# Expert weights in a ring of sixteen 1 MB slots, expert loops unrolled by four, and the slot pick moved behind the transposes of the hidden layer

## The reference

```
gt  = min(x @ w_gate[e] + b_gate[e], 7)
up  = clip(x @ w_up[e] + b_up[e], -7, 7)
out = ((up + 1) * gt * sigmoid(1.702 * gt)) @ w_down[e] + b_down[e]
```

## Time and profile before

| | |
|---|---|
| runs | 1501.61, 1501.67, 1499.98 us; median 1501.61 |
| the profiled execution | 1499.89 us, of which the span is 1498.0 us |
| PE busy | 1383.3 us (92%), 6703 instructions |
| DVE, ACT busy | 584.5 us (39%), 287.7 us (19%) |
| mean granted TensorE clock | 0.948 of 2.4 GHz |
| DMA | 445.40 MB, mean 297 GB/s; expert weights 192 DMAs of 2048 KB |

### The profile page before, as it was taken

One profiled execution on the slowest core, in us unless ns is written; L12 is line 12 of the kernel. 1 busy time (PEld: TensorE's weight loads), 2 busy tenths in 40 slices (PEclk: granted clock), 3 DMA queues, 4 the chain that ended last, 5 costly groups with the idle time before them and its releaser, 6 DMA issues.

```text
span 1498.0 us, 18536 instructions
## 1 busy us (share of the span) xinstructions
PE 1383.3 (92%) x6703; PEld 598.1 (40%) x6704; DVE 584.5 (39%) x1195; ACT 287.7 (19%) x484; POOL 4.0 (0%) x24
## 2 busy tenths in 40 slices
PE   7997778997699999999999999999999999999993
PEld 5886565686233333333333333333333333333331
DVE  2998687311433233433334233412333332222231
ACT  2132222012112212212112212111112211121111
POOL 0000000000000000000000000000000000000000
PEclk9999787598799999999999999999999999999996
DMA  9343112233099999999999999976899998777550
GB/s 395 145 183 120 56 44 109 102 154 137 10 412 417 414 399 400 416 415 416 405 392 416 417 415 401 416 300 262 351 414 417 415 415 339 280 313 301 217 233 30
DMA packets 35404, 445.40 MB, mean 297 GB/s; under 512 B 4904, under 2 KB 5288, under 8 KB 8624
## 3 DMA queue, kind: packets, MB, share of 16 engines
q1 hardware_dynamic: 33760, 443.20, 72.1%
q10 hardware_dynamic: 1616, 1.82, 0.3%
HBM read 437.80 MB, written 7.20 MB: 297 GB/s over the span
## 4 chain that ended last, share of the span: by engine, by line
PE 81%; DVE 10%; DVEq 3%; issue 3%; ACT 2%; DMA 0%; ACTq 0%
PE ps L1203 51%; PE ps L1180 6%; PE ps L1213 6%; DVE acts L586 5%; PE ps L986 3%; PE ps L1193 2%; DVEq L587 2%; PE ps L1102 2%; PE ps L1146 2%; PE ps L1086 2%; PE ps L1093 1%; PE ps L1010 1%; PE ps L1220 1%; ACT extra L513 1%; PE ps L1064 1%
## 5 line engine op out<-in xcount | busy, mean ns | idle before, releaser
L1203 PE MATMUL ps<-ring,extra 128*64 128x512 f32 x3360 | 778.7, 604 | 0.0
L1203 PEld LDWEIGHTS ps<-ring,extra 128*64 128x64 f32 x3360 | 223.0, 137 | 447.5 <-issue 447.5
L901 DVE TENSOR_TENSOR acts<-ps,acts 128x528 f32<-128x528 f32 x132 | 93.4, 708 | 511.9 <-PE ps L1213 511.9
L1180 PE MATMUL ps<-acts 128*64 128x512 f32 (+1 forms) x432 | 105.4, 607 | 2.9 <-issue 2.9
L518 ACT ACTIVATE extra<-extra 128x512 f32<-128x512 f32 x64 | 39.4, 630 | 352.7 <-DVE extra L906 352.7
L1213 PE MATMUL ps<-acts,extra 64*128 64x264 f32 x576 | 100.7, 433 | 4.5 <-DVE acts L901 2.4
L586 DVE SCALAR_TENSOR_TENSOR acts<-acts,small 128x256 f32<-128x256 f32 x240 | 102.7, 479 | 5.1 <-ACT acts L401 0.7
L1213 PEld LDWEIGHTS ps<-acts,extra 64*128 64x128 f32 x576 | 44.6, 186 | 112.0 <-issue 107.4
L529 ACT ACTIVATE extra<-ps 128x512 f32<-128x512 f32 x64 | 34.7, 594 | 249.4 <-PE ps L1203 249.4
L513 ACT ACTIVATE extra<-ps 128x512 f32<-128x512 f32 x66 | 36.2, 595 | 221.6 <-PE ps L1180 221.6
L1010 PE MATMUL ps<-acts,ring 128*128 128x280 f32 (+1 forms) x320 | 77.2, 401 | 0.3 <-DVE acts L661 0.3
(11 more groups left out here) (243 smaller groups left out, 823.3 us busy)
## 6 DMA issues: line engine op xcount, KB each, us to landing
ring<-in_w_experts SPq DMA_DIRECT2D x192, 2048.0 KB, 12.2
ring<-in_w_in_t SPq DMA_DIRECT2D x5, 2048.0 KB, 21.0
extra<-in_w_in_t SPq DMA_DIRECT2D x4, 2048.0 KB, 11.1
ring<-in_state_t SPq DMA_DIRECT2D x8, 512.0 KB, 17.4
extra<-in_w_out_t SPq DMA_DIRECT2D x4, 1024.0 KB, 5.9
ring<-in_w_out_t SPq DMA_DIRECT2D x4, 1024.0 KB, 5.8
out_ssm_s_t<-ring SPq DMA_DIRECT2D x8, 512.0 KB, 2.6
acts<-in_x_cm SPq DMA_DIRECT2D x2, 560.0 KB, 5.8
```

The costliest lines, as they stand in the source:

```text
L901: TT(both, ps[:, 6:8, 0:TN], both, ALU.add).then_inc(ev["acc_done"], 1)
L1180: h = MM(dst, S[0:r, j, HALF * b:HALF * (b + 1)], xn[0:r, j, 512 * h_:512 * (h_ + 1)], start=(j == 0), stop=(j == 2))
L1203: hs.append(MM(dst, src[:, o:o + HALF], piece(p)[:, k, 512 * h_:512 * (h_ + 1)], start=(fresh and kk == 0), stop=(kk == KT - 1), skip_grou ...
```

## The change

- SBUF is laid out anew: `ring` and `acts` become one tensor `main`; the router's tables, `gfin` and the like move from `acts` to `small`, so that the first 32 KB of `acts` are free for four more slots once the mixer is over. The twelve pieces of an expert now go round sixteen slots: piece p of an expert with i mod 4 = s lies in slot (12 s + p) mod 16. Loads keep their trigger events, but go four pieces further ahead; the first two pairs of expert 1 are loaded with expert 0's last ones.
- As slots depend on i mod 4, the expert loops of TensorE and SP have four experts in their body (8 passes on TensorE; SP: 7 passes and 3 experts written out).
- TensorE: `pick_slots` goes from between up pieces 5 and 6 to between `turn_hidden` and `turn_following`. The wait for `xg_out` is by block, and `down_of` waits for it too.
- ScalarE: the order is `inputs_out` b, `hidden_out` b for b = 0, 1, then `gates_out`. VectorE: `hidden` comes before `Pm`.
- POOL's iota waits for `wo_used` instead of two earlier events.

```diff
-        NP = 12
-        ring = sb("ring", NP * PIECE)
+        NP, SLOTS = 12, 16
+        main = sb("main", NP * PIECE + 16400)
+        ring, acts = main, main[:, NP * PIECE:NP * PIECE + 16400]
         extra = sb("extra", 4 * PIECE)
-        acts = sb("acts", 16400)
-        small = sb("small", 4000)
+        small = sb("small", 4040)
...
+        def slot_of(s, p):
+
+            return (NP * s + p) % SLOTS
...
+            sp.wait_ge(ev["yvar_mm"], 1)
+            for q in range(2):
+                sp.dma_start(pair_row(6 + q), expert_pair(1, q)).then_inc(landed[6 + q], 16)
...
-            with sp.Fori(0, NE - 1) as i:
-                sp.wait_ge(ev["gate_used"], i + 1)
-                for q in range(2):
-                    sp.dma_start(pair_row(q), expert_pair(i + 1, q)).then_inc(landed[q], 16)
-                for q in range(2, NP // 2):
-                    sp.wait_ge(ev["piece_used"], i * 8 + 2 * q - 2)
-                    sp.dma_start(pair_row(q), expert_pair(i + 1, q)).then_inc(landed[q], 16)
+            def load_next(e, s, last=False):
+
+                for q in range(2, 6):
+                    if q < 4:
+                        sp.wait_ge(ev["gate_used"], e)
+                    else:
+                        sp.wait_ge(ev["piece_used"], e * 8 + (2 * q - 14))
+                    pair = slot_of(s, 2 * q) // 2
+                    sp.dma_start(pair_row(pair), expert_pair(e, q)).then_inc(landed[pair], 16)
+                if not last:
+                    for q in range(2):
+                        sp.wait_ge(ev["piece_used"], e * 8 + (2 * q - 2))
+                        pair = slot_of(s + 1, 2 * q) // 2
+                        sp.dma_start(pair_row(pair), expert_pair(e + 1, q)).then_inc(landed[pair], 16)
+
+            with sp.Fori(0, NE // 4 - 1) as ii:
+                for s in range(1, 5):
+                    load_next(ii * 4 + s, s)
+            for e in range(NE - 3, NE):
+                load_next(e, e % 4, e == NE - 1)
...
             with a.Fori(0, NE) as i:
                 sigmoid(i * 2)
+                for b in range(2):
+                    inputs_out(i * 2 + 2, b)
+                    hidden_out(i * 2, b)
                 gates_out(i)
-                inputs_out(i * 2 + 2)
-                hidden_out(i * 2)
                 output_out(i)
...
                 choose_slots(i + 2).then_inc(ev["s_ready"], 1)
+                hidden(i, i * 2)
                 v.wait_ge(ev["gp_ready"], i + 1)
                 for b in range(2):
                     h = STT(Pm[:, b, :], ps[:, 6, 0:TN], slot_id[:, b:b + 1], gp, ALU.is_equal, ALU.mult)
                 h.then_inc(ev["p_ready"], 1)
                 choose_bias(i + 2).then_inc(ev["oh_ready"], 1)
-                hidden(i, i * 2)
...
-                    if p == 5:
-                        pe.wait_ge(ev["acc_done"], n4 + 4)
-                        pick_slots()
...
                         if p == 8:
                             pe.wait_ge(ev["ht_ready"], i2 + 1 + b)
+                            pe.wait_ge(ev["xg_out"], i2 + 3 + b)
...
-                by_width(count, lambda n: up_of(n, i * 16 + 16, i * 4))
+                def turn_following(n):
+                    for b in range(n):
+                        pe.wait_ge(ev["xg_out"], i * 2 + 3 + b)
+                        if b:
+                            pe.wait_ge(ev["hdn_ready"], i * 2 + 2)
+                    turn(n, xg, 2, ev["xt_done"])
+
+                by_width(former, lambda n: gate_of(n, s, i48, former_rows))
+                by_width(count, lambda n: up_of(n, s, i48))
                 pe.wait_ge(ev["s_ready"], i + 2)
-                by_width(following, lambda n: gather(n))
+                by_width(following, gather)
                 by_width(count, lambda n: turn_hidden(n, i * 2))
-                pe.wait_ge(ev["xg_out"], i * 2 + 4)
+                pe.wait_ge(ev["acc_done"], i * 4 + 4)
+                pick_slots()
                 by_width(following, turn_following)
-                by_width(count, lambda n: down_of(n, i * 2, i * 16 + 16))
-                pe.wait_ge(ev["ht_ready"], i * 2 + 2)
+                by_width(count, lambda n: down_of(n, i * 2, s, i48))
+
+            with pe.Fori(0, NE // 4) as ii:
+                for s in range(4):
+                    expert(ii * 4 + s, s, ii * 48)
+                pe.wait_ge(ev["ht_ready"], ii * 8 + 8)
```

More of the change, by code:

```diff
@@ L146, in build @@
         rstd3 = sm(TN)
-        eps_c = sm(1)
-        assert so[0] <= 4000, so[0]
+        assert so[0] <= 4040 and route + 1150 + D <= 4040, so[0]
         xrstd = sgt[:, 1, :]
@@ L177, in build @@
[L177 to L185, removed]
+        brow = view(acts, 8192, D)
+        Pm, gp = view(acts, 9216, 2, TN), view(acts, 9744, TN)
@@ new lines, in build @@
+        SG = view(acts, 10008, TN)
+        S = view(acts, 10272, 3, CAP)
+        oh, pick, slot_id = view(acts, 10656, HALF), view(acts, 10720, NE + 2), view(acts, 10754, 2)
+        iota_f = view(acts, 10756, P)
+        xn = view(acts, 10928, 3, D)
+        c0 = route
+        slotp, gates = view(small, c0, 3, NE + 2), view(small, c0 + 102, 3, NE + 2)
+        logit, top8 = view(small, c0 + 204, 3, NE), view(small, c0 + 300, 3, 8)
+        topf, topw = view(small, c0 + 324, 3, TOPK), view(small, c0 + 336, 3, TOPK)
@@ new lines, in build @@
+        eq, mask = view(small, c0 + 348, TOPK, NE), view(small, c0 + 476, 3, NE)
+        tmp96 = view(small, c0 + 572, 3, NE)
+        cntf, nbo, cum = view(small, c0 + 668, NE), view(small, c0 + 700, NE), view(small, c0 + 732, NE)
+        ole, oe, ob = view(small, c0 + 764, OVER, NE), view(small, c0 + 1020, OVER + 1), view(small, c0 + 1029, OVER)
+        oslot = view(small, c0 + 1037, 3)
+        topi = view(small, c0 + 1040, 3, 8).bitcast(U32)
+        otab = view(small, c0 + 1064, OVER + 1).bitcast(I32)
@@ L188, in build @@
+        zero32 = view(small, c0 + 1073, NE)
+        cnti = view(small, c0 + 1111, NE + 2).bitcast(I32)
+        rsum, nmax = view(small, c0 + 1105, 3), view(small, c0 + 1108, 3)
+        gfin = view(small, c0 + 1150, D)
+        hout = view(main, 0, 3, D)
+        hsq = view(extra, 0, D)
         names = ("consts x_lo x_hi vec_loaded sq_a sq_v stat_mm xr_ready uT_ready win_done gsig_ready glu_done csmp_loaded xsmp_loaded "
@@ L197, in build @@
         ev = {n: sem(n) for n in names}
-        landed = [sem(f"pair_landed{i}") for i in range(NP // 2)]
+        landed = [sem(f"pair_landed{i}") for i in range(SLOTS // 2)]
         win_landed = [sem(f"win_landed{i}") for i in range(5)]
@@ L222, in wout_row, with piece, pair_row @@
             return view(ring if q < 4 else extra, (16384 if q < 4 else 0) + (q % 4) * PIECE, PIECE)
[L224 to L228, removed]
+        def slot_of(s, p):
+            return (NP * s + p) % SLOTS
+        def piece(slot):
+            return view(main, slot * PIECE, 2, D)
+        def pair_row(pair):
+            return view(main, 2 * pair * PIECE, 2 * PIECE)
         expert_w = I["w_experts"]
@@ L508, in _, with inputs_out @@
             act(stat[:, 3, 0:3], stat[:, 0, 0:3], ACT.Copy).then_inc(ev["topexp"], 1)
[L510 to L513, removed]
+            def inputs_out(i2, b):
+                a.wait_ge(ev["xg_done"], i2 + 1 + b)
+                act(xg[:, 512 * b:512 * (b + 1)], ps[:, 4 + b, :], ACT.Copy).then_inc(ev["xg_out"], 1)
             def sigmoid(i2):
@@ L519, in sigmoid, with hidden_out @@
                         ).then_inc(ev["sig_ready"], 1)
[L521 to L524, removed]
+            def hidden_out(i2, b):
+                a.wait_ge(ev["ht_done"], i2 + 1 + b)
+                act(hT_e[:, 512 * b:512 * (b + 1)], ps[:, b, :], ACT.Copy).then_inc(ev["ht_ready"], 1)
             def output_out(n):
@@ L546, in _ @@
                 with a.If(j < n_over):
[L547 removed]
+                    inputs_out(j * 2 + 2 * (NE + 1), 0)
+                    inputs_out(j * 2 + 2 * (NE + 1), 1)
                     sigmoid(j * 2 + 2 * NE)
+                    hidden_out(j * 2 + 2 * NE, 0)
+                    hidden_out(j * 2 + 2 * NE, 1)
                     gates_out(j + NE)
[L550 removed]
                     output_out(j + NE)
@@ L1247, in _, with gate_of @@
             pe.wait_ge(ev["rows_loaded"], 32)
-            def gate_of(n, i16, then):
+            def gate_of(n, s, i48, then):
                 for p in range(4):
-                    _, h = piece_products(p, 0, xT, 0, False, i16)
+                    _, h = piece_products(p, 0, xT, 0, False, s, i48)
                     if p == 3:
@@ L1284, in down_of, with expert @@
                             pe.wait_ge(ev["ht_ready"], i2 + 1 + b)
-                        _, h = piece_products(p, b, hT_e, 4, True, i16)
+                            pe.wait_ge(ev["xg_out"], i2 + 3 + b)
+                        _, h = piece_products(p, b, hT_e, 4, True, s, i48)
                     h.then_inc(ev["piece_used"], 1)
-            with pe.Fori(0, NE) as i:
+            def expert(i, s, i48):
```

(2 more changed lines are left out.)

57 lines of the change are left out of this document (18 added, 39 removed).

## The result

The changed kernel takes 1534.81 us (median of four runs, 1531.46 to 1548.58) against 1501.64 for the kernel before (median of four beside them): a ratio of 1.020, 95% interval 1.0145 to 1.0255. It is slower by about 2%, where 2.2% faster was forecast. The profiled execution took 1534.21 us, with a span of 1532.3.

What follows compares the result with a forecast made beforehand. PE was taken as the bound, at 30.52 us per narrow expert, with DMA right behind. 1499.9 less 25.4 (pick and waits) less 6.8 (clock drops) gave 1467.6 us, range 1462 to 1486.

Steps and rivals of the forecast that it cites:

- items 1 and 2: Slot pick moved from the up pieces to behind the first transposes, ending ScalarE's wait: 0.95 us saved per narrow expert.
- item 3: Count over the experts: 26 narrow ones save 24.7 us, three ahead of wide ones 0.2 each; together 25.4 us.
- item 5: Weight ring of sixteen slots: no wait for weights to remove, saves nothing; lets the DMA run on where idle.
- item 6: VectorE's and ScalarE's new order: 4 to 5 us of work covered by the down pieces' 7.02; costs nothing.
- item 7: Unrolled expert loops: each backward jump costs 0 to 4.7 us, taken as 0.
- item 4: Clock in the down pieces: four half-clock drops behind the 0.70 us ScalarE wait vanish, saving 6.8 us.
- the clock drops stay: Rival on the down pieces' clock: half-clock drops persist without the wait; 1474.4 us, chance 0.13.
- the one of the backward jumps: Rival at the unrolled loop's end: seven jumps not hidden, 17 to 33 us, 1485 to 1500; chance 0.11.
- The rival on the slower side: Rival on weight loads: refetched code packets of the unrolled body delay them; 1486 to 1518 us, chance 0.06.

Runs made afterwards that it cites:

- e7: e1 with TensorE's 32 experts written out, no loop, still on twelve slots; 1487.2 us, ratio 0.984 to 0.992.
- e6: e2 with the weight loads of experts 1 to 31 cut to 64 KB each, output not the reference's; 1540.1 us, one run.
- e3: The changed kernel with TensorE's experts written out 32 times, no loop or backward jump; 1492.6 us, ratio 0.987 to 0.996.
- e1: Kernel before with only the pick's new places and ScalarE's and VectorE's new orders; twelve slots, loops kept; 1485.1 us, ratio 0.981 to 0.992.
- e2: Kernel before with only TensorE's expert loop unrolled by four, twelve slots, old places; 1566.7 us, ratio 1.035 to 1.047.
- e4: e1 with TensorE's expert loop unrolled by two; 1615.6 us, ratio 1.067 to 1.079.
- e8: e1 with the pick moved, in wide experts, into the wait between first and second block's transposes; 1483.9 us, ratio 0.977 to 0.993.
- e5: e1 with a never-entered block of 120 products (31 KB of code) behind the down pieces; 1484.2 us, one run.
- e9: e1 again with more rounds; 1484.9 us, ratio 0.987 (0.982 to 0.992).

## Why the prediction was wrong

**Right.** What bounds the kernel (TensorE, with the DMA just behind), items 1 and 2 (0.92 us saved per narrow expert, 0.95 forecast; no wait for ScalarE left), the count of item 3 (26 narrow experts), item 5 (sixteen slots worth nothing, e7; a faster DMA pace of 421 to 425 GB/s that was there all along) and item 6 (no cover lost).

**The step that failed is item 7**, the backward jumps, taken at 0. Measured: seven idle stretches, 39.4 us in all, and 17.5 us of half clock behind them. Three parts of it:
- That the four-fold body would be fetched anew in each pass was seen as open; it is so (117 packets between 432 and 1460 us).
- The bound was too low. "At most 4.7 us" came from idle times of two engines behind the last expert. A jump's branch takes 6 to 7.5 us while weights are loaded (e6: 3.5 us with hardly any). The row used as nearest was taken at a time when the DMA was idle. The branch's own row would have shown the stall itself, if not its later size: the line of that skipped loop, in the kernel before, has a branch of 3.6 us among those of 0.2:

```profile
L1328 PEldq COMPARE_BRANCH  x8: 219/221/3642, 1471.2 to 1480.0; - x8
```

- The cover was overrated. The argument for 0 was that the present loop hides three value loads and a jump, and its first pass the packets. Both hold, but they show only that the sequencer is more than 2.8 us ahead; it is 3.8 to 4. The first pass's packets were read in sequence, which says nothing about a jump (nor are branches out of that sequence free: in e3 the sequencer stands at forward ones for up to 4.0 us, just within its lead). The reading of that pass was also a little off: from bias product to bias product it took 32.17 us, not 30.52. The 1.65 us more are half clock in its first products, not a wait for code, so the conclusion stood. The page's figure for the queue, "Advanced Engine Details and Errata" of the Trainium skill, section "Engine Queue Depths" (64 instructions), led to an estimate that 4.7 us would be covered; here the sequencer was 3.8 us ahead, by the jump's start at 511.6 and the products' end at 515.4.

**A cost that no item had**: behind each idle stretch TensorE loses another 2.5 us at the half clock (17.5 in all). The prediction had read the same effect behind a wait of 0.7 us (item 4) and not asked it of its own 4.7 us. Item 4 says, too, that no other part of an expert shows the lower level; the first expert does, behind a wait of 2.49 us:

```profile
395.71 1.20 PE L1193 MATMUL ps<-acts 32*64 32x512 f32 x8 [2.49 <-DVE extra L893]
396.84 3.47 PE L1203 MATMUL ps<-ring,extra 128*64 128x512 f32 x8
```

**Item 4** was half right. The four drops behind the 0.7 us wait did vanish, but the sum over the stage didn't: 6.8 us went and 8.8 came elsewhere, in the changed kernel and, with 9.7, in e1, around the wide experts, where the pick was now added to a wait that stays. The rival "the clock drops stay" had the better case by its own reason, since it named the wide experts. Item 3's 0.2 us per expert ahead of a wide one did not come (33.55 us against 33.50). The forecast's own sum is 1467.7, not 1467.6, which changes nothing.

**The rival that happened** is the one of the backward jumps, given a chance of 0.11 and 17 to 33 us. It was right in its place and too cheap: 56.9 us with the clock. The rival on the slower side was another mechanism, and e3 rules it out. At 8.1 us a jump, seven jumps are more than twice the 21.9 us that the rest of the change saves (56.9 - 35.0). The turning point lay at 32 / 7 = 4.6 us a jump by the forecast's savings, and at 21.9 / 7 = 3.1 by the measured ones.

**What stays open**: why the branch takes 7.2 us in the changed kernel and 6.2 in e2 (the deeper ring isn't needed for it: e4, on twelve slots and with the new places, has 7.5), why e2 and e6 have a branch of 7.1 us behind the last expert that the other runs lack, and where exactly between 90 and 118 KB the store ends.

## What to carry to other kernels

Before unrolling an engine's loop, look whether instruction packets run during it: where there are none, the body lies in the store, and an unrolling that pushes it out can cost more than it saves. Here the branch took 6 to 7.5 us beside the weight loads, the work already handed over hid about 4, and with the loads at the loop's top and the half clock behind, each jump cost 7.6 to 8.4 us. Written out in full, the same code cost nothing, but by a thin margin: stalls of up to 4.0 us at forward branches against a lead of about 4. Where the work ahead of a branch is shorter, look at the branches' own rows. Moving short independent work into a wait paid twice here, since the clock stayed up as well (e8); put beside a wait that stays, it cost twice (e1).

## What the runs showed of the hardware

- TensorE's loop body stays in its store up to at least 90 KB of code and not at 118 KB; a backward branch takes 0.2 us inside and 6.2 to 7.5 us (medians of three kernels) outside of it, 3.5 us with the weight loads cut down. The sizes are those of the built program.
- Code written out, 107 packets of 16 KB beside weights at up to 429 GB/s, cost no measurable time (e3). The sequencer stood at 20 forward branches for 1 to 4.0 us each, under the work already handed over.
- A forward branch over 31 KB not yet fetched took 6.5 us the first time and 0.2 us afterwards (e5).
- The sequencer was 3.8 to 4 us ahead of the end of TensorE's products at the loops' ends, where these are 512 columns wide.
- Idle time of 4.6 to 6.2 us in the changed kernel was followed by half clock each time (7 of 7), that of 1.8 to 2.3 us in e6 in the next gate piece in 4 of 7 cases, that of 0.7 us in 4 of 26 cases before, that of 1.25 us in none of 3 before and, with more short work behind it, in all 3 of e1.
- The mixer ahead of the experts, unchanged, lasted between 395 and 409 us from one execution to the next, at a granted clock of 0.86 (before) and 0.82 (e8). Between the profiled executions of e1 and e9, the same kernel, it makes the whole difference: 401.4 against 396.8 us ahead of the stage, 1485.2 against 1480.6 in all.
